# Reordering the first tiles of a SwiGLU: hidden-value stores before the next weight loads, hidden sums before down-weight sums, one low part later

## What is computed

```python
def swiglu_ffn(h, w_gate, w_up, w_down):        # h 1024x1024, w_gate and w_up 1024x2816, w_down 2816x1024
    return (jax.nn.silu(h @ w_gate) * (h @ w_up)) @ w_down
h = rms_norm(x, ffn1_norm_g[l])
x = x + 0.5 * swiglu_ffn(h, ffn1_w_gate[l], ffn1_w_up[l], ffn1_w_down[l])
```

## Time and profile before

| | us |
|---|---|
| median of three timed runs | 1928.9 (1927.47 to 1931.25) |
| the profiled execution, its own time | 1928.37 |
| its span in the trace | 1926.8 |
| TensorE busy | 1894.0 (98%) |
| VectorE busy | 1107.8 (57%) |
| ScalarE busy | 675.5 (35%) |
| GpSimd busy | 416.5 (22%) |
| mean granted TensorE clock | 0.998 of full |

### The profile page before, as it was taken

How to read it: one execution, slowest core, us unless ns; L and a number is a source line. 1 busy time by engine, 2 the same in 40 slices (tenths; PEclk the granted TensorE clock), 3 DMA queues, 4 the chain that set the end, 5 groups by cost and what they waited for, 6 DMA issues and landing times.

```text
span 1926.8 us, 24683 instructions
## 1 busy us (share of the span) xinstructions
PE 1894.0 (98%) x9384; PEld 1570.6 (82%) x9384; DVE 1107.8 (57%) x1491; ACT 675.5 (35%) x1027; POOL 416.5 (22%) x322
## 2 busy tenths in 40 slices
PE   9899999999999999999999899999999999999999
PEld 7688888888888888888888667887888888888887
DVE  6866666665556641145545774357756666655564
ACT  7332323333333533211221764264232323333332
POOL 2322432241103010002202320002323422321030
PEclk9999999999999999999999999999999999999999
DMA  5454535446865433313331610044444454458653
GB/s 167 147 177 146 176 132 187 145 148 228 323 197 194 126 134 123 129 55 131 131 113 62 222 59 1 23 131 143 157 171 162 145 171 152 147 214 327 215 190 141
DMA packets 220365, 295.77 MB, mean 154 GB/s; under 512 B 14545, under 2 KB 117081, under 8 KB 220257
## 3 DMA queue, kind: packets, MB, share of 16 engines
q1 hardware_dynamic: 206752, 262.19, 39.8%
q0 software_dynamic: 5152, 16.85, 2.7%
q10 hardware_dynamic: 8352, 15.27, 2.1%
HBM read 205.37 MB, written 91.51 MB: 154 GB/s over the span
## 4 chain that ended last, share of the span: by engine, by line
PE 91%; DVE 3%; issue 2%; ACT 2%; DMA 1%; POOL 1%; SPq 0%; DVEq 0%; ACTq 0%; POOLq 0%
PE ps L699 28%; PE ps L701 28%; PE ps L700 28%; PE ps L901 3%; PE ps L733 1%; PE ps L999 1%; PE ps L986 1%; PE ps L1019 1%; DVE S L1996 0%; DMA rawx<-ffn_w_down 0%; PE ps L922 0%; DMA xs<-x 0%; PE ps L892 0%; PE ps L925 0%; PE ps L915 0%
## 5 line engine op out<-in xcount | busy, mean ns | idle before, releaser
L699 PE MATMUL ps<-hThi,whi 128*128 128x512 f32 x896 | 351.3, 392 | 9.8 <-DVE hid L1683 8.0
L700 PE MATMUL ps<-hTlo,whi 128*128 128x512 f32 x896 | 349.7, 390 | 0.0
L701 PE MATMUL ps<-hThi,wlo 128*128 128x512 f32 x896 | 349.7, 390 | 0.0
L699 PE MATMUL ps<-whi 128*128 128x512 f32 x616 | 240.1, 390 | 0.9 <-DVE wlo L1732 0.9
L700 PE MATMUL ps<-wlo,whi 128*128 128x512 f32 x616 | 239.7, 389 | 0.0
L701 PE MATMUL ps<-whi,wlo 128*128 128x512 f32 x616 | 239.6, 389 | 0.0
L699 PEld LDWEIGHTS ps<-hThi,whi 128*128 128x128 f32 x896 | 168.9, 188 | 46.1 <-issue 10.8
L701 PEld LDWEIGHTS ps<-hThi,wlo 128*128 128x128 f32 x896 | 168.9, 188 | 35.2
L700 PEld LDWEIGHTS ps<-hTlo,whi 128*128 128x128 f32 x896 | 169.0, 189 | 34.7
L1650 DVE TENSOR_TENSOR wlo<-raw,whi 128x512 fp32r<-128x512 f32 x176 | 132.5, 757 | 97.6 <-ACT whi L1213 97.5
L699 PE MATMUL ps<-hXhi,whi 128*128 128x512 f32 x480 | 186.8, 389 | 0.0
(11 more groups left out here) (192 smaller groups left out, 2911.9 us busy)
## 6 DMA issues: line engine op xcount, KB each, us to landing
hid_scratch<-hid SPq DMA_DIRECT2D x132, 256.0 KB, 3.2
raw<-ffn_w_gate SPq DMA_DIRECT2D x44, 512.0 KB, 3.7
raw<-ffn_w_up SPq DMA_DIRECT2D x44, 512.0 KB, 4.9
wdb<-ffn_w_down SPq DMA_DIRECT2D x44, 512.0 KB, 4.1
wd_scratch<-wdb SPq DMA_DIRECT2D x88, 256.0 KB, 4.5
raw<-hid_scratch SPq DMA_DIRECT2D x80, 256.0 KB, 2.8
rawx<-hid_scratch SPq DMA_DIRECT2D x74, 256.0 KB, 2.8
raw<-w_in SPq DMA_DIRECT2D x28, 512.0 KB, 4.8
```

The costliest lines, as they stand in the source:

```text
L699: pe.matmul(dst, ahi, bhi, start=first, stop=False, skip_group_check=onto)
L700: pe.matmul(dst, ahi, blo, start=False, stop=False, skip_group_check=onto)
L701: return pe.matmul(dst, alo, bhi, start=False, stop=last, skip_group_check=onto)
```

## The change

Three things are moved, in both SwiGLU steps; nothing is added or removed.

1. VectorE: the fourth `t34_lo` (j = 3) leaves its place behind the third and stands behind `plain_hid` of tile 0.
2. GpSimd: the hidden sums of pair 0 stand ahead of the down-weight sums of pair 0. The other pairs keep their order.
3. SyncE: what was issued in tile 1 behind the store of A11 (the down-sum stores of pair 0 and `load_down(1)`), and `gate_up(4)` at the head of tile 2, now stand at the end of tile 2: stores of A12, A22 and of the four hidden sums first, then `gate_up(4)`, the down-sum stores, `load_down(1)`.

```diff
             def ffn(F, w_gate, w_up, w_down, x_src):
                 for e in range(FT):
-                    if e + 2 < FT:
+                    if e + 2 < FT and e != NPLAIN:
                         gate_up(F, e + 2, w_gate, w_up)
                     if e == 0:
                         load_down(F, 0, w_down)
                     elif e % 2:
                         store_hid(F, e - 1, A11)
-                        store_down_sums(F, e // 2)
-                        if e // 2 + 1 < NPAIR:
-                            load_down(F, e // 2 + 1, w_down)
+                        if e > NPLAIN:
+                            store_down_sums(F, e // 2)
+                            if e // 2 + 1 < NPAIR:
+                                load_down(F, e // 2 + 1, w_down)
                     else:
                         store_hid(F, e - 1, A12)
                         store_hid(F, e - 1, A22)
                         for i in (S3, S1, S2, S4):
                             store_hid_sum(F, e // 2 - 1, i)
+                    if e == NPLAIN:
+                        gate_up(F, e + 2, w_gate, w_up)
+                        store_down_sums(F, 0)
+                        load_down(F, 1, w_down)
...
                 if e < NPLAIN and i == 7:
                     plain_hid(F, e)
+                    if e == 0:
+                        t34_lo(F, 3)
...
-            for j in range(4):
+            for j in range(3):
                 t34_lo(0, j)
...
-            for j in range(4):
+            for j in range(3):
                 t34_lo(1, j)
...
             def ffn(F):
-                for k in range(NPAIR):
+                hid_pair_sums(F, 0)
+                down_sums(F, 0)
+                for k in range(1, NPAIR):
                     down_sums(F, k)
                     hid_pair_sums(F, k)
```

## The result

| | before | after |
|---|---|---|
| median of 20 runs each, us | 1930.57 | 1934.34 |
| the profiled execution's own time, us | 1928.37 | 1933.01 |
| its span, us | 1926.8 | 1931.4 |
| TensorE's mean granted clock | 0.998 | 0.996 |

The ratio of the times is 1.0023, with a 95% interval from 1.0016 to 1.0030, some 4.4 us; the two medians differ by 3.8. The forecast was +0.9 us within 1923.0 to 1933.4, so the time lies 0.9 us above the range, and in "slower" (above 1932.8), which had a chance of 0.14. The median of the kernel before is itself 1.7 us higher over 20 runs than over the three that were known.

A forecast was written before the change was run, and what follows sets the result against it. TensorE, busy 98% of the span, was taken as the bound, so only its idle or slow stretches could give time. Terms -2.0 + 2.9 + 0 = +0.9 us on 1928.37 gave 1929.3, as median 1929.8; range 1923.0 to 1933.4.

The forecast's parts named there:

- The place: TensorE would idle about 5 us before product 6 of tile 2 in both SwiGLUs, waiting for `up1`.
- the mechanism: Ahead of `up1`, no store wait; six GpSimd instructions crowd VectorE, 1.10 us each, less 0.6: 6.0 us.
- (2, 0) at 65.8 with no gain: First SwiGLU: product 0 of tile 2 starts 1.14 us earlier, but TensorE only arrives at its next stall earlier.
- One sign of being wrong: Gaps of GpSimd ahead of S2 or S4 of over 2 us would point to rival 2.
- rival 2: Partly crowded: late landings let two down sums per SwiGLU end after VectorE passed; -6.2 us, 1922.7; chance 0.13.
- tile 3, taken as 0: Later down sums of pair 1 were taken to cost tile 3 nothing, because it has slack on VectorE.
- The part on SyncE's reordering: Down-sum stores of pair 0 wait until 85.8, `down_sums(1)` runs from about 94 instead of 88.1; cost taken as 0.
- The clock, counted as even: Two stalls of 5.1 and 5.0 us, each worth 0 or 2.7 us; one lowered clock, as before: difference 0.
- rival 4: Slower: a 5 us stall in the second SwiGLU, both stalls lower the clock; +3.6 us, 1932.5, up to 1934; chance 0.20.
- first SwiGLU, start of (2, 6): Product 6 of tile 2 starts at 87.6 instead of 89.55, 2.0 us earlier.
- second SwiGLU, idle time before (2, 6): TensorE's idle time before product 6 of tile 2 grows from 2.09 to 5.0 us: +2.9 us.
- Rival 1: The stalls before product 6 of tile 2 vanish, GpSimd and VectorE not hindering each other: -9.8 and -2.1 us, 1917; chance 0.10.

The follow-up runs named there:

- two variants: Changed kernel without the fourth low part's move, ratio 1.0020 to before; changed kernel with tile 3's gate and up loads ahead of the first down load, ratio 1.0027.
- the last kernel: Kernel before with SyncE's reordering, weights 15 to 18 behind `up1`, and the second low part moved behind `plain_hid` of tile 0: 1918.48 us, ratio 0.9940.

## Why the prediction was wrong

**What held.** The place (L1688 before (2, 6) in both SwiGLUs), the mechanism (no store any more, VectorE crowded at 1.7 us for an instruction), (2, 0) at 65.8 with no gain, the sign of both terms. The forecast put VectorE at L1683 at 86.7 and 1351.5; it came at 87.79 and 1350.40. One sign of being wrong did show, and meant little: GpSimd stood 3.15 us ahead of S2 in the first SwiGLU (over 2 us, rival 2), but VectorE waited for its load just as long, so all six instructions still fell in.

**The step that failed: tile 3, taken as 0.** The part on SyncE's reordering bounded the later `down_sums(1)` by 0 and 4.4 us and took 0, since TensorE had waited for L1683 only twice in the whole trace. That row is about `up1` in tiles where VectorE has caught up with TensorE. Here VectorE leaves (2, 6) late, and the next sums fall on its way to L1702 of tile 3. It cost 0.92 us in the profiled execution, 1.9 us in each SwiGLU in two variants, and the experiment without these sums got 4.2 us back.

**Terms mis-sized.** The first SwiGLU gave 0.94 us at the start of (2, 6) and not 2.0. The up load took 8.3 us and not 6.8, and the store of A11 8.3 and not 6.3: VectorE started `weight_sums` at 76.44 instead of 75.0. The forecast carried one landing time, from one trace, to another kernel, where the same load takes 6.8 to 9.4 us over the traces here. That was worth about 1 us. The second SwiGLU's idle time grew by 2.43 us and not 2.9.

**The clock, counted as even.** The forecast took one lowered clock in two stalls, against one before, as a difference of 0. Both stalls, 6.25 and 4.52 us, lowered it, as rival 4 had it. (2, 6) lasted 4.6 us each time, 1.8 more than at full clock each, against 2.7 once: +0.9 us. Each stall before (2, 6) of 3.73 us or more in the other kernels lowered it too, and none of 2.62 us or less did; but the wait of 2.00 us before (2, 3) in the last kernel did, so the length of the idle time alone doesn't tell it.

**The sum with what was measured** (us, from the two profiles):

| term | forecast | measured |
|---|---|---|
| first SwiGLU, start of (2, 6) | -2.0 | -0.9 |
| second SwiGLU, idle time before (2, 6) | +2.9 | +2.4 |
| low clock in (2, 6), both | 0 | +0.9 |
| tile 3 | 0 | +0.9 |
| sum | +0.9 | +3.3 |

The sum missed by 2.4 us: 0.9 each for tile 3 and the clock, 0.6 for landings and turns. The ratio's interval is 3.1 to 5.8, so the sum lies within it, at its lower end; the span's 4.6 are, to 0.1, these 3.3, less the 1.2 that the wait in the trace of before is worth, and 2.6 more for the low clock in the attention stretch. What is left between 3.3 and the 4.4 of all executions is open: it can be tile 3 (0.92 in this profile, 3.8 in two variants), or how often the clock falls elsewhere. The outcome is that of rival 4 (1932.5, up to 1934), with a chance of 0.20, plus the seam to tile 3. The range ended at 1933.4, which left out the end of rival 4, and tile 3 was no term of it. Against a median of before that was 1.7 us low from three runs, 4.4 us would have been 1933.3, just within it, so part of the miss of the range is that.

**The rivals.** Rival 1 (stalls vanish) came true for a part of the change: SyncE's reordering alone is 8.2 us faster. The forecast weighed the three edits as one and never asked for the best subset, though its own steps said that the store was the releaser, that the low part held the loads back and that the down sums crowd VectorE.

## What to carry to other kernels

When a stall's releaser is removed, count what stands ahead of the waiting instruction in its own engine's order, and which other engine's work slows that queue meanwhile; here the stall passed from a store to VectorE's queue at nearly the same length. An instruction that is moved by one microsecond takes along everything that waits for its semaphore: ask of a moved instruction first who else waits for it. And price each edit of a change by itself, down to the point where the engine behind has caught up again: one of three was worth 0.43%, the other two together cost 0.66%, each of them most of it by itself.

## What was not expected of the hardware

Matmuls that compute nothing, 24 in each of two stalls, made the changed kernel faster by 0.23%; the granted clock of 1.00 in both (2, 6) is worth 3.4 us of that, two times 1.7. The clock fell once after a wait of 2.00 us and stayed at 1.00 after waits of 2.57 and 2.62.

And the up load of tile 3, 512 KB, landed 6.8 us after its issue in the first SwiGLU of the kernel before, 7.2 with only the low part late, 8.3 in the changed kernel, behind the same three loads each time. The two or three stores that follow at once in the changed kernel look like the cause, but they follow in its second SwiGLU too, where the load took 6.8 us, and in the same place of the kernel with busy matmuls it took 9.4; with SyncE's reordering and two weights later, where A11's store follows after 1.1 us and the next only after 4.9, it took 8.4. What sets it is open.
